# Experts of a mixture: rows grouped by expert in 32-row slots instead of by group in 128-row windows, and weights used as plain fp32

## The reference, cut to what matters

```python
def hierarchical_moe(x, w_rg, b_rg, w_re, b_re, w_g, w_u, w_d):
    # n = 256 rows, 4 groups of 8 experts, D = 1024, D_EXPERT = 256
    g_prob = softmax(xt @ w_rg + b_rg);  g_val, g_idx = top_k(g_prob, 1)
    e_logit = (xt @ w_re + b_re)[chosen group];  e_prob = softmax(e_logit)
    e_val, e_idx = top_k(e_prob, 2);  e_val = e_val / sum(e_val)
    comb[n, g, e] = g_val * e_val            # zero for all but two experts of one group
    for g in range(4):
        hg = silu(einsum('nd,edf->nef', xt, w_g[g])) * einsum('nd,edf->nef', xt, w_u[g])
        y = y + einsum('nef,efd->nd', hg * comb[:, g, :, None], w_d[g])
```

## Time and profile before

| | us |
|---|---|
| median of three runs | 2080.56 |
| the profiled execution, its own time | 2080.89 |
| its span, first to last instruction | 2079.0 |
| PE busy in the span | 1926.9 (93%) |
| DVE busy | 1553.0 (75%) |
| ACT busy | 1146.6 (55%) |
| POOL busy | 12.9 (1%) |
| DMA engines, share of the span | 57.6% |

### The profile page before, as it was taken

How to read it: one execution, slowest core, us unless ns; L and a number is a source line. 1 busy time by engine, 2 the same in 40 slices (tenths; PEclk the granted TensorE clock), 3 DMA queues, 4 the chain that set the end, 5 groups by cost and what they waited for, 6 DMA issues and landing times. The chain is left out here.

```text
span 2079.0 us, 29959 instructions
## 1 busy us (share of the span) xinstructions
PE 1926.9 (93%) x11440; PEld 1661.1 (80%) x11440; DVE 1553.0 (75%) x1755; ACT 1146.6 (55%) x1254; POOL 12.9 (1%) x18
## 2 busy tenths in 40 slices
PE   7999899979998999699989999999599899999996
PEld 6877799968776999587778898898477678889885
DVE  5958587878676777647758888887558678888886
ACT  4565355535563555335655676675346546677663
POOL 0000000000000000000000000000000000000000
PEclk9999999999999999899999999999799999999998
DMA  6534355545433555254355698896454265889883
GB/s 222 188 122 144 130 185 189 172 156 189 163 113 127 182 190 190 84 197 142 122 170 180 246 350 322 337 363 224 153 162 142 82 209 176 335 321 343 333 332 144
DMA packets 172066, 422.46 MB, mean 203 GB/s; under 512 B 15824, under 2 KB 68408, under 8 KB 155320
## 3 DMA queue, kind: packets, MB, share of 16 engines
q1 hardware_dynamic: 171960, 421.00, 57.6%
HBM read 419.93 MB, written 1.05 MB: 202 GB/s over the span
## 5 line engine op out<-in xcount | busy, mean ns | idle before, releaser
L228 DVE TENSOR_TENSOR w_lo<-raw,w_hi 128x2048 fp32r<-128x2048 f32 (+2 forms) x350 | 782.6, 2246 | 183.1 <-ACT w_hi L223 180.8
L223 ACT ACTIVATE w_hi<-raw 128x2048 fp32r<-128x2048 f32 (+2 forms) x350 | 655.5, 1879 | 187.7 <-PE lot L271 162.7
L269 PE MATMUL lot<-w_hi,two_xw_hi 128*128 128x256 f32 x992 | 289.7, 292 | 8.6 <-DVE w_lo L228 7.6
L271 PE MATMUL lot<-w_hi,two_xw_lo 128*128 128x256 f32 x992 | 278.2, 280 | 0.0
L270 PE MATMUL lot<-w_lo,two_xw_hi 128*128 128x256 f32 x992 | 277.1, 279 | 0.0
L269 PE MATMUL lot<-w_hi,two_hT_hi 128*128 128x512 f32 (+1 forms) x544 | 216.8, 399 | 16.9 <-DVE w_lo L228 15.5
L270 PE MATMUL lot<-w_lo,two_hT_hi 128*128 128x512 f32 (+1 forms) x544 | 212.2, 390 | 0.0
L271 PE MATMUL lot<-w_hi,two_hT_lo 128*128 128x512 f32 (+1 forms) x544 | 212.0, 390 | 0.0
L269 PE MATMUL lot<-one_hT_hi,w_hi 128*128 128x256 f32 x704 | 200.9, 285 | 5.1 <-DVE one_hT_lo L359 5.1
L269 PEld LDWEIGHTS lot<-w_hi,two_xw_hi 128*128 128x128 f32 x992 | 186.5, 188 | 20.4 <-DVE w_lo L228 11.4
L270 PE MATMUL lot<-one_hT_lo,w_hi 128*128 128x256 f32 x704 | 200.7, 285 | 0.0
(11 more groups left out here) (430 smaller groups left out, 3341.7 us busy)
## 6 DMA issues: line engine op xcount, KB each, us to landing
raw<-w_in SPq DMA_DIRECT2D x78, 1024.0 KB, 5.0
raw<-w_exp_gate SPq DMA_DIRECT2D x50, 1024.0 KB, 6.2
raw<-w_exp_up SPq DMA_DIRECT2D x48, 1024.0 KB, 6.5
raw<-w_exp_down SPq DMA_DIRECT2D x46, 1024.0 KB, 5.3
raw<-ffn_w_up SPq DMA_DIRECT2D x44, 1024.0 KB, 5.1
raw<-ffn_w_down SPq DMA_DIRECT2D x22, 1024.0 KB, 5.0
two_fourth<-w_exp_down SPq DMA_DIRECT2D x18, 1024.0 KB, 6.4
raw<-w_out SPq DMA_DIRECT2D x16, 1024.0 KB, 5.7
```

Of the source, the lines that this page charges most:

```text
L223: act.activation(K.hi[:, r, 0:n], self.raw(name)[:, 0:n], ACT.Copy).then_inc(K.sig["hi_ready"], 1)
L228: dve.tensor_tensor(K.lo[:, r, 0:n], self.raw(name)[:, 0:n], K.hi[:, r, 0:n].bitcast(F32), ALU.subtract).then_inc(K.sig["lo_ready"], 1)
L269: pe.matmul(out, a[0], b[0], start=start, stop=False)
L271: return pe.matmul(out, a[1], b[0], start=False, stop=stop)
```

## The change

The rows are grouped by expert. Each expert has 32 slots (CAP), and four experts (a round, `q`, of which there are NQ = 8) share the 128 slots. Per round: a gather of the 128 slots' rows from x (32 products of 128 columns, then plain copies from PSUM); for each expert gate and up as plain fp32 products with 32 stationary columns (`xw[:, k, rows]`) into the expert's own 32 partitions of a lot; one SiLU, one product with a weight per slot and two transposes for all four experts; one down projection per expert, again with 32 stationary columns; a split of the round's output into `y_hi` and `y_lo`; and the turning back as fp32r products with a 0/1 matrix, added to x. The slots of a round come from a rank of each row within each expert, counted by PE over 32 experts. Weights are neither split nor copied: PE reads them where the load puts them, in a ring of 12 slots made of `raw`, `w_hi`, `w_lo` and three other places. The first loads are issued early: three behind the router's weights, the next nine as the slots come free during the gated product. The eight rounds are written out, not looped. `WINDOW_TURN`, `Windows`, POOL's copies and `x_before` go. If one of the experts has over 32 rows, a loop of 7 x 8 more rounds follows, under an If. The rank products now stand behind the last quarter of `pg0`.

With these constants QB = 1, KX = 4, NX = 2.

```diff
@@ constants @@
+CAP = 32
+BE = P // CAP
+QE = 4
+QB = QE // BE
+NQ = N_E // QE
+KX = 512 // (QE * CAP)
+NX = KD // KX
+E_RING = 12
...
@@ TwoTiles @@
+        self.xw = over("xw", [P, KD, QE * CAP], "gates")
+        self.y_hi = over("y_hi", [P, QB, D], "hT_hi", F32R)
+        self.y_lo = over("y_lo", [P, QB, D], "hT_lo", F32R)
+        extra = (over("e_p", [P, CHUNK], "p"), over("e_skT", [P, CHUNK], "skT"), over("e_gates", [P, CHUNK], "gates", off=8 * KB))
+        self.ring = [t[:, :] for t in extra] + [t[:, r, :] for t, r in (
+            (K.raw, 1), (K.raw, 2), (K.plain_hi, 1), (K.plain_lo, 1), (K.raw, 0), (K.plain_hi, 2), (K.plain_lo, 2),
+            (K.plain_hi, 0), (K.plain_lo, 0))]
...
@@ in place of window_chunks, window_ends, window_lots, Windows @@
+def following(q, s):
+    if s + 1 < QB:
+        return q, s + 1
+    return (q + 1, 0) if q + 1 < NQ else None
+def expert_chunks():
+    names = up_chunks(0, 0)
+    for q in range(NQ):
+        for s in range(QB):
+            n = following(q, s)
+            names += (up_chunks(*n) if n else []) + down_chunks(q, s)
...
+    def load_again(self, sp, name):
+        before = self.names[self.at[name] - E_RING]
+        if before in self.ends:
+            self.filled(sp, self.ends[before])
+        else:
+            sp.wait_ge(self.K.sig["e_used"], self.used[before])
+        self.load(sp, name, int(name[1:]))
...
+    def gather(self, pe, q, i=None):
+        K, M = self.K, self.M
+        pe.wait_ge(K.sig["e_rows"], later(q + 1, i, 1))
+        for j in range(NX):
+            name = f"X{q}.{j}"
+            lot = self.claim(pe, name, i)
+            for kk in range(KX):
+                k = KX * j + kk
+                for t in range(T):
+                    for x in (M.x_hi, M.x_lo):
+                        last = pe.matmul(K.ps[1][:, lot - 2, kk * QE * CAP:(kk + 1) * QE * CAP], x[:, t, k * P:(k + 1) * P],
+                                         M.rows01[:, t, :], start=t == 0 and x is M.x_hi, stop=t == T - 1 and x is M.x_lo)
+            last.then_inc(self.L.filled(name), 1)
...
+    def hidden(self, pe, q, s, half, i=None):
+        K, M = self.K, self.M
+        name = f"H{q}.{s}"
+        lot = self.L.use[name][0]
+        if half == 0:
+            for j in range(NX):
+                self.drained(pe, f"X{q}.{j}", i)
+            self.claim(pe, name, i)
+        for j in range(half * BE // 2, (half + 1) * BE // 2):
+            rows = slice((s * BE + j) * CAP, (s * BE + j + 1) * CAP)
+            for bank, c in enumerate("GU"):
+                chunk = f"{c}{QE * q + BE * s + j}"
+                w = self.weights(pe, chunk, i)
+                for k in range(KD):
+                    last = pe.matmul(K.ps[0][j * CAP:(j + 1) * CAP, lot, bank * D_E:(bank + 1) * D_E], M.xw[:, k, rows],
+                                     w[:, k, :], start=k == 0, stop=k == KD - 1)
+                self.done(last, chunk)
...
+    def turn(self, pe, q, s, i=None):
+        K, M = self.K, self.M
+        self.drained(pe, f"H{q}.{s}", i)
+        self.claim(pe, f"T{q}.{s}", i)
+        for f in range(2):
+            last = pe.transpose(K.ps[3][:, 0, f * P:(f + 1) * P], M.act[:, 1, f * P:(f + 1) * P], K.ident[:, :])
+        last.then_inc(self.L.filled(f"T{q}.{s}"), 1)
+    def down(self, pe, q, s, i=None):
+        K, M = self.K, self.M
+        self.drained(pe, f"T{q}.{s}", i)
+        self.claim(pe, f"Y{q}.{s}", i)
+        for j in range(BE):
+            chunk = f"D{QE * q + BE * s + j}"
+            w = self.weights(pe, chunk, i)
+            for n in range(2):
+                for f in range(2):
+                    last = pe.matmul(K.ps[2][j * CAP:(j + 1) * CAP, n, :], M.h[:, f, j * CAP:(j + 1) * CAP],
+                                     w[:, f, n * 512:(n + 1) * 512], start=f == 0, stop=f == 1)
+            self.done(last, chunk)
+    def give(self, pe, q, i=None):
+        K, M = self.K, self.M
+        self.drained(pe, f"W{q}", i)
+        for s in range(QB):
+            self.drained(pe, f"Y{q}.{s}", i)
+        for t in range(T):
+            for n in range(2):
+                name = f"B{q}.{2 * t + n}"
+                lot = self.claim(pe, name, i)
+                for s in range(QB):
+                    for y in (M.y_hi, M.y_lo):
+                        last = pe.matmul(K.ps[1][:, lot - 2, :], M.back[:, s, t * P:(t + 1) * P],
+                                         y[:, s, n * 512:(n + 1) * 512], start=s == 0 and y is M.y_hi,
+                                         stop=s == QB - 1 and y is M.y_lo)
+                last.then_inc(self.L.filled(name), 1)
...
+    def silu(self, act, q, s, i=None):
+        lot = self.filled(act, f"H{q}.{s}", i)
+        if i is None and (q or s):
+            before = (q, s - 1) if s else (q - 1, QB - 1)
+            self.drained(act, f"H{before[0]}.{before[1]}")
+        act.activation(self.M.act[:, 0, :], self.K.ps[0][:, lot, 0:D_E], ACT.Silu).then_inc(self.K.sig["e_silu"], 1)
+    def out_hi(self, act, q, s, i=None):
+        self.filled(act, f"Y{q}.{s}", i)
+        if i is None and q:
+            self.filled(act, f"B{q - 1}.{2 * T - 1}")
+        act.activation(self.M.y_hi[:, s, :], flat(self.K.ps[2][:, :, :]), ACT.Copy).then_inc(self.K.sig["e_out"], 1)
+    def out_lo(self, dve, q, s, i=None):
+        dve.wait_ge(self.K.sig["e_out"], later(q * QB + s + 1, i, QB))
+        dve.tensor_tensor(self.M.y_lo[:, s, :], flat(self.K.ps[2][:, :, :]), self.M.y_hi[:, s, :].bitcast(F32),
+                          ALU.subtract).then_inc(self.L.drained(f"Y{q}.{s}"), 1)
...
+    def adds(self, dve, q, i=None):
+        for t in range(T):
+            for n in range(2):
+                name = f"B{q}.{2 * t + n}"
+                lot = self.filled(dve, name, i)
+                x = self.K.x[:, t, n * 512:(n + 1) * 512]
+                dve.tensor_tensor(x, self.K.ps[1][:, lot - 2, :], x, ALU.add).then_inc(self.L.drained(name), 1)
...
@@ block_two, sync @@
+                if name == "route":
+                    L.wait_filled(sp, "saT3")
+                    E.load(sp, E.names[0], int(E.names[0][1:]))
+                    L.wait_filled(sp, "saS3")
+                    E.load(sp, E.names[1], int(E.names[1][1:]))
+                    sp.wait_ge(sig["merged"], 4)
+                    E.load(sp, E.names[2], int(E.names[2][1:]))
...
+            sp.wait_ge(sig["lo_ready"], ST.ready["pg01"])
+            E.load(sp, E.names[3], int(E.names[3][1:]))
+            sp.wait_ge(sig["lo_ready"], ST.ready["pg10"])
+            E.load(sp, E.names[4], int(E.names[4][1:]))
+            ST.wait_used(sp, "pg01")
+            for name in E.names[5:7]:
+                E.load(sp, name, int(name[1:]))
+            sp.wait_ge(sig["lo_ready"], ST.ready["pg11"])
+            E.load(sp, E.names[7], int(E.names[7][1:]))
+            ST.wait_used(sp, "pg10")
+            for name in E.names[8:10]:
+                E.load(sp, name, int(name[1:]))
+            ST.wait_used(sp, "pg11")
+            for name in E.names[10:12]:
+                E.load(sp, name, int(name[1:]))
+            for name in E.names[E_RING:3 * N_E]:
+                E.load_again(sp, name)
...
@@ block_two, tensor @@
+            E.gather(pe, 0)
+            both("pg0")
+            E.turn_rows(pe, 0)
+            both("rank")
+            E.hidden(pe, 0, 0, 0)
+            E.hidden(pe, 0, 0, 1)
+            if QB == 1:
+                E.gather(pe, 1)
+            for q in range(NQ):
+                for s in range(QB):
+                    n = following(q, s)
+                    if n:
+                        E.hidden(pe, *n, 0)
+                    E.turn(pe, q, s)
+                    if s == 0 and q:
+                        E.give(pe, q - 1)
+                    if n:
+                        E.hidden(pe, *n, 1)
+                        if n[1] == QB - 1 and n[0] + 1 < NQ:
+                            E.gather(pe, n[0] + 1)
+                        if n[1] == 0:
+                            E.turn_rows(pe, n[0])
+                    if q == s == 0:
+                        both("pg1")
+                    E.down(pe, q, s)
+            E.give(pe, NQ - 1)
...
@@ block_two, vector @@
+            E.product(dve, 0, 0)
+            if QB == 1:
+                E.dve_pieces(dve, 1)
+            for q in range(NQ):
+                for s in range(QB):
+                    n = following(q, s)
+                    more = n and n[1] == QB - 1 and n[0] + 1 < NQ
+                    if more:
+                        E.rows(dve, n[0] + 1)
+                    if s == 0 and q:
+                        E.adds(dve, q - 1)
+                        E.back(dve, q)
+                    if n:
+                        if more:
+                            E.dve_pieces(dve, n[0] + 1)
+                        if n[1] == 0:
+                            E.row_weights(dve, n[0])
+                        if more:
+                            E.weigh_rows(dve, n[0] + 1)
```

(51 more changed lines are left out.)

523 lines of the change are left out of this document (222 added, 301 removed).

## The result

The changed kernel takes **2102.86 us** (median of four runs, 2100.45 to 2104.07), against 2080.36 of the kernel before beside it (2078.4 to 2084.83): ratio 1.0104, interval [1.0085, 1.0122]. It is 22.5 us slower, where I forecast 95 us faster. The predicted range holds it, but the time moved the other way than forecast; one rival named it closely: "from 4 passes", 41.1 us a round and 2117.

The account below looks back on a forecast made before the run. PE was taken as the bound, weights second: 31.1 us a round, 33 with coupling, eight rounds ending a stage at 1413.6 instead of 1460.6, 94 us saved over two layers, so 1985 us; range 1905 to 2130, forecast's own 1950 to 2030.

Parts of the forecast that it names:

- from 4 passes: Rival, expert stage: PE picks from only 4 passes, 41.1 us a round, 2117 us, slower than before; chance 0.08.
- 17 passes lie in PE's queue: Gate and up: an expert's passes start when the expert before has 17 left, making a half round 10.3 us, not 13.8.
- the attention product: Masked attention's two heads: 8 passes in 0.88 us, taken to show PE starts later instructions early over at least 4 passes.
- Half stage 10.3: Gate and up of two experts, half of a round of four: 48 steps of 0.215 us, 10.3 us.
- Down projections and the half behind them: Down overlapping about threefold, 5.6 us, then a half stage of 10.3 that begins under its tail, saving 2.7 us.
- changes between forms of work: Five changes a round between whole-array and column-group work on PE, about 0.2 us each, 1.0 us.
- The gate product's load: Three early expert loads delay the ple gate's chunks by 8 us, just covered: landed about 1096, first split at 1104.06.
- The end at 1413.6: End of a layer's expert stage, 1413.6 against 1460.6 before: 47 us saved a layer, 94 in both.
- The turning point: Round length at which the changed kernel turns from faster to slower than the one before: about 39 us.
- The clock rival: Rival, expert stage: PE's clock halves and passes double; a whole stage gives about 55 us a round, 2450 us; chance 0.10.
- Strict order: Rival, expert stage: no overlap beyond neighbouring passes, 48.8 us a round, 2239 us; chance 0.08.
- The weights' rate: Expert weight loads: 12.58 MB a round takes 33.4 us at 376 GB/s, or 30.5 at the best slice's 412.

Follow-up runs that it names:

- runs of 16: Changed kernel with the two experts of a half stage changing places after 16 passes (a chunk) instead of 32: 2051.9 us, ratio 0.9861.
- the versions in turns: Changed kernel with gate and up product by product over four experts, down also in turns 1911.68 us, down unaltered 1919.95; over two experts, down in turns, 1909.55.
- the stretch with the waits for landings: Changed kernel with gate, up and down all in turns over four experts, all weights loaded: 1911.68 us, ratio 0.9185.
- the two that follow it in the text: Changed kernel with gate and up in turns over four experts, down unaltered: 1919.95 us; over two experts, down in turns over four: 1909.55 us.
- halved chunks: Changed kernel with all products in turns over four experts, only the first half of every weight chunk loaded and read twice: 1739.38 us, ratio 0.8359.

## Why the prediction was wrong

**The step that failed** is "So 17 passes lie in PE's queue ... I take 17, the depth that is seen." show how far ahead the sequencer works out registers. That is no proof that passes can start from there: seventeen may be queued, and the head of the queue stands still as soon as its column group is full. The only row in which a pass really started past others was the attention product, and there each head has exactly four passes, one running and three waiting, and the second head's first pass starts 14 ns after the first head's (168.969 and 168.983 us). It could not show more, and I used it as a lower bound where it was the limit itself. The choice between ends far apart should have gone by it, since it was the same operation; instead it went by a register instruction. What the runs showed in its place: a pass can start ahead of others only once all of those ahead of it have found room in their own groups, one running and three waiting in each. So an expert of 32 passes overlaps the next with its last three and not with its last 17, and the half stage takes 13.10 us, not 10.3.

**The terms**, against a round of 40.10:
- Half stage 10.3, measured 13.10: 2.8 too little. Down projections and the half behind them 5.6 + 10.3 - 2.7 = 13.2, measured 20.08: 6.9 too little (down 8.70 for 5.6, the half 13.10 for 10.3, and an overlap of 1.7 for 2.7). With 1.0 for changes between forms of work that no gap shows (PE is idle for 0.3 us in the round), 31.1 + 2.8 + 6.9 - 1.0 = 39.8.
- A pass every 0.215 us at 256 columns and 0.43 at 512: right (0.216, 0.43). Gather 3.6: 3.63. Turning back 2.6: 2.76. Transposes 0.44: 0.52 with the rows' weights.
- DVE 6.7 and ACT 2.4 a round, hidden: right (6.21, 2.39). Rounds for fuller experts: not run. The gate product's load was covered: the gather starts at 1136.6, 2.8 us sooner than before.
- The end at 1413.6: measured 1468.9. The loss is (332.4 - 321.2) + (332.2 - 320.1) = 23.3 us of the 22.5 measured.

**The rivals.** The one of 4 passes came true, at a chance of 0.08: round 41.1 for 40.10, 2117 for 2103. It was right in its mechanism for these long runs, since four passes in hand and the four oldest passes come to nearly the same there. The turning point, "about 39 us a round", is confirmed: runs of 16 with 36.77 are faster than before, 40.10 is slower. The clock rival fell: 1.00 in the round. Strict order (48.8 a round) fell as well, but it was nearer to the truth in kind than my forecast: the trace with `gates` at 1147.28 ahead of `skT` at 1147.49 speaks against "strict FIFO" in "TensorE: Matmul & The Clock Gate" of the Trainium skill, section "Part 3: Packing small matmuls — row/col tiling", yet passes are handed out in order, and only the room in each group, three passes, lets them start out of it.

**The weights' rate** was taken too low, 376 to 412 GB/s; full, the DMA engines reach 417 to 418 over 100 us, 12.58 / 0.4175 = 30.1 us a round. It cost the forecast nothing, since PE was the bound, but sets the time of the versions in turns. "Perfetto Trace Analysis" of the Trainium skill, section "Roofline", has it so: a core that is alone may go above its share of 358 GB/s and is held by its DMA engines at about 435; the runs agree, with 417 to 418 over 100 us and 427 at best.

## What to carry to other kernels

Column groups work side by side only if the program's order brings each its next pass while no group has more than four in hand: with fp32 products as here, change the group after each product, and never write one group's whole contraction before the next one's. Here that order alone, with the same passes and bytes, was worth 193 us of 2103, and turned a change that lost 1% into one that gains 8%. And when a depth is wanted, take it from passes seen to start out of order, not from how far a sequencer has read.

## What the runs showed of the hardware

- Each 32-column group of PE behaved as if it held one running pass and three waiting ones, and the next pass for it stopped the hand-out for all groups. All of this is fp32, where each pass has a weight load of its own (in the round above 205 of either), so whether passes or their loads are counted can't be told. The length of a pass doesn't matter: with 512 columns (runs of 8 down passes) the same rule gives 20 x 0.43 = 8.6 us, and the down projections of the changed kernel take 8.70 (the first starts at 1201.57, the last at 1209.84, and 0.43 for its step). The next half stage began under them at 1208.56, which is why the two together took 20.08.
- Four groups at once cost nothing in the pace of each: 0.216 and 0.43 us a pass, whether one group works or four.
- In the stretch with the waits for landings, PE 74 us of 100 busy, the mean granted clock was 0.90, so for part of it PE ran at 1.2 GHz; in the two that follow it in the text 0.95 and 0.98. None of it is seen in the time, which the weights set: 1911.68 us at 0.90, 1909.55 at 0.98.
- The 16 DMA engines moved 417 to 418 GB/s over 100 us in chunks of 1 MB, share 1.02; with halved chunks 360 GB/s at share 0.98, which I had not expected. Whether the smaller chunks or the shorter supply of free slots set that rate was not tried.
